# Stick-breaking attention: the end values copied by ScalarE, the first output sum one step later, the last mean-square transposes before the projection products

## The reference, cut to what matters

```
z       = (q . k) * dh**-0.5                      # per head, query t, key s < t
log_not = where(s < t, log_sigmoid(-z), 0)
after   = reverse_cumsum(log_not) - log_not
w       = where(s < t, exp(log_sigmoid(z) + after), 0)
o       = w @ v
```

## Time and profile before

| | us |
|---|---|
| median of 3 runs (lowest, highest) | 2128.99 (2128.32, 2129.59) |
| the profiled execution's own time | 2129.34 |
| its span, first to last instruction | 2127.6 |
| TensorE busy in the span | 2053.3 (97%) |
| VectorE busy | 1255.7 (59%) |
| GpSimd busy | 783.0 (37%) |
| ScalarE busy | 683.6 (32%) |
| stick-breaking stage | from about 551 to 1172 of the span |

### The profile page before, as it was taken

How to read it: one execution, slowest core, us unless ns; L and a number is a source line. 1 busy time by engine, 2 the same in 40 slices (tenths; PEclk the granted TensorE clock), 3 DMA queues, 4 the chain that set the end, 5 groups by cost and what they waited for, 6 DMA issues and landing times. The chain is left out here.

```text
span 2127.6 us, 29374 instructions
## 1 busy us (share of the span) xinstructions
PE 2053.3 (97%) x9904; PEld 1677.1 (79%) x9904; DVE 1255.7 (59%) x2001; ACT 683.6 (32%) x1212; POOL 783.0 (37%) x697
## 2 busy tenths in 40 slices
PE   5999999999999999999998999987999999999999
PEld 4888888887777777777776788876888888888887
DVE  5758686753467667667667546467444444444444
ACT  3434243311334334334335100026222233322232
POOL 3423132322221122122111333358555555555552
PEclk8999999999999999999999999998999999999999
DMA  4212121222442342342453522111111111110112
GB/s 124 49 30 60 30 59 25 65 67 79 103 102 42 93 100 53 84 108 54 74 143 134 210 86 89 59 59 41 59 60 59 59 59 59 39 59 21 58 59 79
DMA packets 137872, 153.94 MB, mean 72 GB/s; under 512 B 7712, under 2 KB 112160, under 8 KB 137824
## 3 DMA queue, kind: packets, MB, share of 16 engines
q1 hardware_dynamic: 136096, 150.17, 25.9%
q10 hardware_dynamic: 1728, 3.15, 0.4%
HBM read 107.16 MB, written 20.97 MB: 60 GB/s over the span
## 5 line engine op out<-in xcount | busy, mean ns | idle before, releaser
L125 POOL TENSOR_TENSOR w_hi<-w_raw,w_ones 128x64 fp32r<-128x64 f32 x88 | 32.7, 372 | 1021.8 <-PE sb_g L151 470.3
L129 POOL TENSOR_TENSOR w_lo<-w_raw,w_hi 128x512 fp32r<-128x512 f32 x176 | 241.9, 1396 | 7.3
L925 DVE TENSOR_TENSOR sb_wt_lo<-sb_t,sb_wt_hi 128x512 fp32r<-128x512 f32 (+2 forms) x186 | 103.1, 554 | 109.7 <-ACT sb_wt_hi L748 108.7
L151 PE MATMUL sb_g<-h_hi,w_hi 128*128 128x512 f32 x544 | 152.8, 409 | 2.7 <-DVEq L799 1.9
L151 PE MATMUL sb_g<-h_lo,w_hi 128*128 128x512 f32 x544 | 150.5, 401 | 0.0
L151 PE MATMUL sb_g<-h_hi,w_lo 128*128 128x512 f32 x544 | 150.1, 400 | 0.0
L748 ACT CAST sb_wt_hi<-sb_t 128x512 fp32r<-128x512 f32 (+2 forms) x186 | 89.8, 483 | 168.4 <-PE sb_t L614 167.8
L151 PE MATMUL gla_g<-h_hi,w_hi 128*128 128x512 f32 x480 | 129.7, 406 | 3.2 <-DVEq L1405 3.2
L151 PE MATMUL gla_g<-h_lo,w_hi 128*128 128x512 f32 x480 | 127.7, 399 | 0.0
L151 PE MATMUL gla_g<-h_hi,w_lo 128*128 128x512 f32 x480 | 126.5, 397 | 0.0
L2070 POOL TENSOR_TENSOR ff_w_lo<-raw_g,ff_w_hi 128x512 fp32r<-128x512 f32 x66 | 85.2, 1290 | 109.7 <-ACT ff_w_hi L2186 109.7
(11 more groups left out here) (385 smaller groups left out, 4935.1 us busy)
## 6 DMA issues: line engine op xcount, KB each, us to landing
w_raw<-w_in SPq DMA_DIRECT2D x64, 512.0 KB, 8.2
raw_g<-w_ffn_gate SPq DMA_DIRECT2D x11, 1024.0 KB, 5.4
ff_raw_u<-w_ffn_up SPq DMA_DIRECT2D x11, 1024.0 KB, 5.8
ff_raw_d<-w_ffn_down SPq DMA_DIRECT2D x11, 1024.0 KB, 4.9
sb_qs<-sb_q_st SPq DMA_DIRECT2D x32, 256.0 KB, 5.1
sb_kh<-sb_k_st SPq DMA_DIRECT2D x32, 256.0 KB, 5.0
sb_kl<-sb_k_st SPq DMA_DIRECT2D x32, 256.0 KB, 5.0
mp_sig<-gates_t SPq DMA_DIRECT2D x16, 512.0 KB, 4.4
```

What stands on the lines that cost most here:

```text
L125: self.nc.gpsimd.tensor_tensor(hi[:, 0:64], raw[:, 0:64], self.ones[:], ALU.mult)
L129: ins = self.nc.gpsimd.tensor_tensor(lo[:, at], raw[:, at], hi[:, at], ALU.subtract)
L151: ins = nc.tensor.matmul(acc, a[:, k, :], b[:, k, half * HALF:(half + 1) * HALF], start=(n == 0), stop=(n == len(steps) - 1))
L925: nc.vector.tensor_tensor(wt_lo[:, m % 2, a:HALF], weight_bank(m, last)[:, a:HALF], wt_hi[:, m % 2, a:HALF], ALU.subtract).then_inc(lo_rea ...
```

## The change

Three edits, all in `stick_breaking`.

1. `take_ends` goes from VectorE to ScalarE, from the end of a pass (and the preparation before the loop) to slot 2 of the pass that uses the values, ahead of that slot's sigmoid. It waits for the same semaphore as before.
2. VectorE's `sum_o` of group (0, 0) goes from slot 10 to slot 11: behind `wt_low` of column 4 and the first part of `k_root`.
3. 17 is taken out of `MS_AFTER`: on TensorE the last mean-square transposes stand ahead of slot 17's `fill` and scores, not behind them. On VectorE the matching `copy_ms` goes ahead of slot 17's `row`.

```diff
-MS_AFTER = [10, 13, 17]
+MS_AFTER = [10, 13]
+MS_EARLY = 17
+ENDS_SLOT = 2
+FIRST_SUM_SLOT = 11
...
+                def take_ends(it):
+
+                    act.wait_ge(o_free, 4 * it + 1)
+                    for e in range(2):
+                        nc.scalar.copy(ends[:, e, :], vt[e * SB_DH:(e + 1) * SB_DH, P::P]).then_inc(ends_ready, 1)
+
                 def body(it, last):
                     for s in range(SLOTS):
                         m, done = step_in(s), step_in(s - 1)
+                        if s == ENDS_SLOT:
+                            take_ends(it)
                         if m is not None:
                             wt_high(it, m, last)
...
-                def take_ends(prep):
-
-                    dve.wait_ge(o_free, 4 * prep + 1)
-                    for e in range(2):
-                        nc.vector.tensor_copy(ends[:, e, :], vt[e * SB_DH:(e + 1) * SB_DH, P::P]).then_inc(ends_ready, 1)
...
-                take_ends(0)
...
                         if m is not None:
                             wt_low(it, m, last)
+                        if s == MS_EARLY and not last:
+                            copy_ms(1, 1, g_uses(it) + 3)
                         if s - 1 in SCORE_SLOT:
                             row(it, SCORE_SLOT.index(s - 1))
...
-                            if s in MS_SLOT:
+                            if s in MS_SLOT and s != MS_EARLY:
...
-                        if done is not None and WEIGHT_STEPS[done][2] == 4 * WEIGHT_STEPS[done][1] + 3:
+                        if s == FIRST_SUM_SLOT:
+                            sum_o(it, 0, 0)
+                        elif done is not None and WEIGHT_STEPS[done][2] == 4 * WEIGHT_STEPS[done][1] + 3 and done > 3:
                             sum_o(it, *WEIGHT_STEPS[done][:2])
...
                     if not last:
                         low_v(it + 1, 1)
-                        take_ends(it + 1)
```

## The result

The changed kernel takes 2138.28 us (median of 5, 2136.91 to 2142.11) against 2128.99; the ratio is 1.0044, with a 95% interval of 1.003 to 1.0057. It is slower, by 9.3 us, and the interval leaves out 1. Forecast were 2136.0 us and a range of 2129.5 to 2143. The profiled execution took 2136.91 us, its span 2135.2.

The account below looks back on a forecast made before the run. TensorE, busy 97% of the span, was taken as the bound; -6.8 - 3.6 + 13.3 + 4.2 = +7.1 us on 2129.34 gave 2136.4, and 2136.0 for the runs' median, range 2129.5 to 2143.

Parts of the forecast that it names:

- Part 1: At the third score block of passes 1 to 6, TensorE's 0.9 us wait for VectorE's running product goes: -6.8 us.
- Part 2: In slot 11, the low part of column 4 starts 0.61 us earlier; 0.45 us per pass remain, -3.6 us.
- The sum follows; the next instruction starts 1.04 after it: On VectorE, the moved first sum follows the root step ending at 657.05, so column 5's low part starts at 658.09.
- the lower bound that I had given: For the moved first sum in slot 11: no gain, if its later place costs as much as it gives.
- Part 3: In slot 17, the moved mean-square transposes wait 2.39 us for `low_q`; net 1.90 us per pass, +13.3 us.
- The wait before the spread: TensorE's 0.29 us wait at 678.03 for the mean-square reduction, priced 0.49 us, would be removed.
- The rival of later waits that absorb the new one: Slots 18 to 24: TensorE's later waits on VectorE absorb slot 17's wait; 2123.0 us, chance 0.08.
- The clock: After slot 17's new wait, three of seven passes lose the granted clock at 1.4 us each: +4.2 us.
- The rival that the clock is never lowered: After slot 17's new waits the granted clock holds in all passes: +2.9 us, 2131.9 us, chance 0.22.
- The estimate from two waits on either side: Clock 1.00 after a 1.93 us wait, 0.83 after 2.40; the new gap of about 2.2 lies between: three of seven.

Follow-up runs that it names:

- parts 1 and 2: The kernel before with the end-value copies moved to ScalarE and the first sum moved to slot 11, mean-square transposes left in place; 2123.2 us, ratio 0.997.
- part 1 alone: The kernel before with only `take_ends` moved to ScalarE in slot 2; 2122.7 us, ratio 0.9965.
- part 3 alone: The kernel before with only the last mean-square transposes and their reduction moved ahead in slot 17; 2152.05 us, ratio 1.0102, and 2153.66 us when run again.

## Why the prediction was right, and where it was not

**Part 1: right.** Forecast were 1.13 us in passes 1 to 6; measured 1.05 (78.65 - 77.60), that is the gap of 0.90 plus 0.15. The copies take 0.42 us for an estimate of 0.43, and the running product ran beside GpSimd in its usual 0.41 us, which the rows of before could not show. That is what the Trainium skill (SBUF — State Buffer, "Who interferes with whom") has: a VectorE instruction that does not need the shared port pair is not held; the trace agrees. What I did not say is that VectorE could have kept the copies in another place.

**Part 2: wrong.** The step that failed is "The sum follows; the next instruction starts 1.04 after it". The 1.04 held (658.46 to 659.50); what did not is that the sum follows at once. It started 0.38 us after the root step's end. Put behind the low part instead, it starts without a gap, so it is the place that costs. I take the 0.38 us for the sum's own four semaphore waits, which are passed only once the root step's last result is there. The rows of the changed kernel fit this: the root step's instructions follow each other after 0.04 us (657.86 to 657.90), a low part with one wait of its own starts 0.13 behind the root step's last (661.85 to 661.98, its high part ready since 661.58), the sum with four 0.38. No run took the waits away, so it is argued and not shown. Before, they stood in VectorE's 0.27 us of idle for ScalarE.

Where the gain went shows in pass 1 of parts 1 and 2 against part 1 alone, each counted from its pass's start. The transposes of column 5 come 0.55 us sooner, where 0.6 were forecast. The multiply of column 4 comes 0.45 sooner, for it now waits for the sum; the prediction had it standing later than the sum's end. The transposes of column 6 come 0.31 sooner, for the low part of column 5 is late, and the score block behind them 0.07. Only a loss at this last place was in the forecast, as 0.15. The measured worth is 0.05 us per pass, near the lower bound that I had given; forecast were 3.6 us in all.

**Part 3: right, in mechanism and size.** Forecast were a gap of about 2.2 us and +1.90 per pass; measured 2.15 and +1.73 (79.30 - 77.57). The wait before the spread went, as forecast. The 1.73 are 2.31 for the new wait less 0.58 that the new order gains; forecast were 2.39 and 0.49. The rival of later waits that absorb the new one is out but for 0.1 to 0.2 us.

**The clock: right in kind, loose in size.** Forecast were three passes of seven at 1.4 us; measured two and four, at 1.57 each (80.87 - 79.30). The rival that the clock is never lowered is out. The estimate from two waits on either side was fair for this kernel, and would have been far too low for part 3 alone, with seven.

**The sum.** A pass at full clock was forecast at 78.97 us and took 79.30. By measured terms, the seven passes of the loop should have grown by -6 x 1.05 - 7 x 0.05 + 7 x 1.73 + 2 x 1.57 = 8.6 us in the profiled execution. They grew by 558.34 - 549.44 = 8.9 (551.28 to 1109.62 against 550.93 to 1100.37), and the whole span by 2135.2 - 2127.6 = 7.6; outside the loop the changed kernel is 1.3 us shorter, which none of the terms explains. The forecast took the gains of parts 1 and 2 for 3.7 us more than they were (0.5 and 3.2), and the costs of part 3 and of the clock for 2.3 more (1.2 and 1.1). These errors cancel but for 1.4 us, which is luck, and so is a part of the rest, as the clock's term differs from execution to execution. That the kernel gets slower, and by which wait, was seen; that 2136.0 came so close to 2138.28 is in part luck.

## What to carry to other kernels

Before an instruction is moved ahead on the engine that sets the time, find the end of the chain that produces its operands, and move the producers too: the same move cost 1.73 us per pass without them and gained 0.58 with them. When a small instruction holds up a critical one, first look for a place where it is not held itself, or where nobody waits behind it; another engine may not be needed. An instruction with several semaphore waits can cost more behind one whose result the engine waits for than behind one that is still running; it was seen here at one place, and is worth a look at the gap in the trace.

## What the runs showed of the hardware that was not expected

- A wait of TensorE of 2.15 us, the same in every pass, is followed by a granted clock of 0.5 (1.2 GHz instead of 2.4) in some passes and not in others: 2 and 4 of 7 in two executions of the changed kernel, 7 and 7 of 7 in two of part 3 alone. It drops after the wait, when TensorE works again, and a fall costs 1.57 us (80.87 against 79.30). Waits of 1.4 us brought none in seven passes.
- So the price of part 3 depends on the rest of the kernel: 16.4 us on top of parts 1 and 2 (9.3 slower against 7.1 faster than the kernel before), and 21.7 by itself (2152.05 against 2130.31), of which by an estimate the clock is 7 x 1.57 = 11.0 if a fall costs the same there.
- A wait of TensorE cost its gap plus 0.16 us at two lengths (2.15 and 1.42 us).
- The same instruction, with four semaphore waits of its own, started 0.38 us late behind an instruction whose result had been waited for, and not late at all behind one whose result had not.
